# Alternating the two token halves between their banks in the dense stage

## The chip, the cores and the metric

The kernel runs on one core of a Trainium2 chip. TensorE multiplies, ScalarE and VectorE read its results out of eight accumulation banks (PSUM, 512 columns of f32 each), GpSimd and SyncE do side work and start DMAs. The metric is the time of one execution in microseconds, the median of several runs. Less is better.

## The reference

A batch of 256 tokens of 1024 values passes two transformer blocks. Cut to the matrix products and what stands between them:

```
h = x @ w_in                                   # first block: nine parts, 9216 columns
ua, va, za, qh, kh, vh, zb, ga, gb = split(h)
ya = gelu(ua) * mix(layer_norm(gelu(va))) * silu(za)
yb = rms_norm(diff_attention(rope(q), rope(k), v)) * silu(zb)
merged = sigmoid(ga) * (ya @ w_branch_a) + sigmoid(gb) * (yb @ w_branch_b)
ple = sigmoid(x @ w_ple_gate) * (p @ w_ple)
x = layer_norm(ALPHA * x + merged @ w_out + ple)

h = rms_norm(x) * (1 + scale_m) + shift_m      # second block
proj = h @ w_in_2                              # latents, fq, fk, fv, gates
merged = sigmoid(gate_a) * (o_mla @ w_o_mla) + sigmoid(gate_b) * (o_fox @ w_o_fox)
x = x + gate_m * (merged @ w_out_2)
h = rms_norm(x) * (1 + scale_f) + shift_f
x = x + gate_f * (shared(h) + routed(h))       # 64 experts, six for each token
return rms_norm(x)
```

All is float32, and the result is to hold that precision.

## The kernel before

The program has two stages. The dense stage does everything up to the last `x = x + gate_m * ...`. The expert stage behind it streams the weights of 64 experts, 3 MB each, and multiplies each with the few tokens that were routed to it.

The dense stage goes by names, each a product of all 256 tokens with 512 columns of a weight matrix (424 for c0): q0 q1 k0 k1 v0 v1 za0 za1 ua0 ... pg0 pg1 ple0 ple1 ba0 ba1 bb0 bb1 wo0 wo1 c0 fq fk fv g0 ... of0 of1 om0 om1 wp0 wp1. A weight matrix comes in loads of four blocks of 128 rows into a ring of five slots, and each load is cut into pieces of two blocks (list `pieces`). So a name of 1024 rows has four pieces, of0, of1, om0 and om1 have two, and ple0 and ple1 one each.

For float32 precision both operands are split in a high and a low part. ScalarE rounds a piece into its high part (`hl`, six buffers), VectorE subtracts to get the low part (`rlo`, in the slots' room). Three matmuls, here called passes, make one block of rows: high tokens by high weights, low tokens by high weights, high tokens by low weights. The tokens are the stationary operand, 128 at a time, so there are two halves, m = 0 and m = 1, each with a bank of its own. One piece for one half is six passes; a step is one piece for both halves, twelve passes.

The order of steps is in `steps_of`. Most names have both halves of a piece in one step. In the runs named in `BEHIND` (bb0 bb1, wo0 wo1, c0, om0 om1, wp0 wp1) the second half comes four (om: three) pieces behind the first. In such a run of eight pieces the steps 0 to 3 hold the first half alone, steps 4 to 7 both halves with different pieces, and steps 8 to 11 the second alone. c0 with its four pieces never has both in one step, and the om run has both in step 3 alone.

TensorE's part is `project`. A name's banks are `bank_of[name] + m`: names take the pair of banks 0, 1 and the pair 2, 3 in turn. Before its first piece a name waits until the name two before it has been emptied from the same bank (`two_before`, `evacuated`). After the last pass of each half of a step TensorE raises the counter `pe_w`; `pe_at` has its value for each piece and half. These wait on that counter:

- the emptying of a bank, by ScalarE (`keep`) or VectorE (`evac`), which waits for a half's last piece (`done`)
- the conversions, which wait for the second half of the piece six before (`both(g - NH)`)
- the loads, which wait for the second half of the last piece of the slot's load (`freed`)

VectorE and ScalarE have their own `project` functions. Each goes through its program in a fixed order, conversions and emptyings mixed, so an emptying can stand behind a conversion that is not ready. In the lagged runs VectorE empties a bank as soon as its name is done and goes on with what follows from it: for wo1 the layer norm, whose result TensorE needs for the transposing products `h_turn(0)`; for bb1 and om1 the sum (`merged`, `merged2`) that TensorE transposes within the run; for wp1 the sum and scale that `h3_turn(0)` transposes.

ple0 and ple1 are emptied by VectorE, by the function `ple`: for each half a product (a tensor_tensor from the bank) and then an addition (a scalar_tensor_tensor from `rbuf` to `rbuf`). The name ba0 comes two behind ple0 and takes its banks.

Of the kernel before, what the change touches and what calls it, by code (L numbers as in the profile page):

```python
# [76 lines left out]
def two_blocks(nc, D, out):  # L77
    ctx = ExitStack()
    with ctx:  # L79
        def sem(name):  # L80
            return ctx.enter_context(nc.semaphore(name))
# [81 lines left out]
        PS = [ctx.enter_context(nc.psum_tensor(f"ps{i}", [128, 512], F32)) for i in range(8)]  # L163
# [13 lines left out]
        def tok(m):  # L177
            return slice(128 * m, 128 * m + 128)
# [36 lines left out]
        loads, pieces, blocks, once = [], [], {}, {}  # L215
# [76 lines left out]
        for name in order:  # L292
# [3 lines left out]
            if name == names[0]:  # L296
                ps = [g for q in names for g in blocks[q]]
                steps_of[name] = []
                for s in range(len(ps) + lag):
                    t = sum(len(v) for v in steps_of.values())  # L300
                    halves = [(ps[s], 0)] if s < len(ps) else []
# [6 lines left out]
        block_of = {g: (name, n) for name in order for n, g in enumerate(blocks[name])}  # L308
# [3 lines left out]
        bank_of = {name: 2 * (n % 2) for n, name in enumerate(order)}  # L312
        two_before = {name: order[n - 2] if n > 1 else None for n, name in enumerate(order)}

        def hi_of(g):
            return hl[:, g % NH, 0:2 * pieces[g][2]].rearrange("p (k n) -> p k n", k=2)
# [50 lines left out]
        hi, lo, pe_w, mac = (sem(n) for n in ("hi", "lo", "pe_w", "mac"))  # L367
# [25 lines left out]
        def evacuated(name, m):  # L393
            ev = ev_v if (name, m) in ev_v.at else ev_a
            return ev.sem, ev.at[(name, m)]
# [422 lines left out]
        def _(e):  # L818
            w = Waits(e)

            def mm(o, l, r, start, stop):
                return e.matmul(o, l, r, start=start, stop=stop)  # L822

            def tr(o, i):
                n = i.shape[0]
                return e.transpose(o, i, ident[0:n, 0:n])  # L826
# [43 lines left out]
            def mod_sum(c):  # L870
                kind, h = c // 2, c % 2
                acc = macc[:, h, :]
                b = take(("mod", c))
                w.wait_ge(mac, 15 * in_turn.index(c) + 15)
                w.wait_ge(ones_set, 1)
                if kind in (2, 5):
                    x = mm(b[:, :], ones[:, :], acc, True, True)
                elif kind in (0, 1):
                    for f in range(4):
                        x = mm(b[:, f:f + 1], acc[:, 128 * f:128 * f + 128], ones[:, 0:1], True, True)  # L880
                else:
                    for k in range(8):
                        x = mm(b[64 * h:64 * h + 64, k:k + 1], acc.rearrange("p (q k) -> p k q", k=8)[:, k, :],
                               ones[:, 0:1], True, True)
                taken(x)

            def between(name, n):
                if n < len(HEADS_IN.get(name, ())):
                    head(HEADS_IN[name][n])
                for n0, s in PAIRS_IN[name][n] if name in PAIRS_IN else ():  # L890
                    pair(n0, s, 96 if n0 else 66, V2 if n0 else FV)

            def project(lead, L, ready, at={}):
                for name in names_of[lead]:
                    for c in MOD_SUM.get(name, ()):
                        mod_sum(c)
                four = len(blocks[lead]) == 4
                for s, (_, halves) in enumerate(steps_of[lead]):
                    for g, m in halves:
                        w.wait_ge(hi, g + 1)  # L900
                        w.wait_ge(lo, g + 1)
                        hi_g, lo_g = hi_of(g), pieces[g][3]
                        name, n = block_of[g]
                        o = PS[bank_of[name] + m][:, 0:pieces[g][2]]
                        if n == 0 and two_before[name]:
                            w.wait_ge(*evacuated(two_before[name], m))
                        for k in range(2):
                            kk = 2 * n + k
                            ready(m, kk)
                            mm(o, L[:, 0, kk, tok(m)], hi_g[:, k, :], kk == 0, False)  # L910
                            mm(o, L[:, 1, kk, tok(m)], hi_g[:, k, :], False, False)
                            x = mm(o, L[:, 0, kk, tok(m)], lo_g[:, k, :], False, kk == 2 * len(blocks[name]) - 1)
                        x.then_inc(pe_w, 1)
                    if s == 1 and four:
                        between(lead, 0)
                    if s in at:
                        at[s]()
                between(lead, 1 if four else 0)
# [76 lines left out]
            for name in ("q0", "q1", "k0", "k1", "v0"):  # L995
                project(name, L0, x_ready)
            turn("qT", lambda m, j: ROT[:, m, 128 * j:128 * j + 128], lambda m, j0: w.wait_ge(roped, 2))
            for name in ("v1", "za0"):
                project(name, L0, x_ready)
            turn("kT", lambda m, j: ROT[:, m, 128 * j:128 * j + 128], lambda m, j0: w.wait_ge(roped, 4))  # L1000
            for name in ("za1", "ua0", "ua1", "va0", "va1", "zb0", "zb1"):
                project(name, L0, x_ready)
            wsT = slot(once["wsT"])[:, 0:1024].rearrange("p (g t) -> p g t", g=8)
            for m in range(2):
                for c in range(2):
# [3 lines left out]
                    for j in range(4):  # L1009
                        g = 4 * c + j  # L1010
                        x = mm(b[:, 128 * j:128 * j + 128], wsT[:, g, :], VA[:, m, 128 * g:128 * g + 128], True, True)
# [24 lines left out]
            for m in range(2):  # L1036
                b = take(("lT", m))
                w.wait_ge(lat_set, 1)
                for j in range(3):
                    x = tr(b[:, 128 * j:128 * j + 128], PR[:, m, 128 * j:128 * j + 128])  # L1040
# [1547 lines left out]
```

## Time and profile before

| | us |
|---|---|
| median of 3 runs | 1091.11 |
| lowest and highest | 1090.81, 1092.13 |
| the profiled execution | 1089.95 |
| its span, first to last instruction | 1088.2 |
| TensorE busy | 1033.8 (95%) |
| VectorE busy | 563.1 (52%) |
| ScalarE busy | 394.3 (36%) |

The span is what the trace shows; the profiled execution is 1.75 us longer than it. Matmuls overlap: the next starts before the one ahead of it has ended, so their pace is read from the distance of their starts. The granted clock of a stretch is a share of TensorE's 2.4 GHz: 1.00 or 0.50. Accumulation banks stand as `ps` in all rows of the trace, without their number.

### The profile page before, as it was taken

How to read it: one execution, taken by the hardware profiler on the slowest of the kernel's cores; microseconds unless marked ns; L12 is line 12 of the kernel's file. 1: busy time of each engine (PE TensorE's matmuls, PEld its weight loads, DVE VectorE, ACT ScalarE, POOL GpSimd, SP SyncE). 2: the span in 40 equal slices, each digit the busy share in tenths (PEclk: the TensorE clock that was granted, in tenths of full speed). 3: DMA queues.
4: the chain of work that ended last, by engine and by line, in shares of the span. 5: the costliest groups of instructions: out<-in, count | busy, mean ns of one | idle time of the engine just before them, and what ended most of it. 6: DMA issues, size and time to landing. Idle time of an engine off the chain costs nothing. (4 is left out here: it accounts for less than half of the span.)

```text
span 1088.2 us, 12949 instructions
## 1 busy us (share of the span) xinstructions
PE 1033.8 (95%) x5024; PEld 688.3 (63%) x5024; DVE 563.1 (52%) x1018; ACT 394.3 (36%) x678; POOL 387.3 (36%) x309
## 2 busy tenths in 40 slices
PE   8999998999999899999999999999999899999993
PEld 7888886878788787788877444444444344444351
DVE  5899678676976876666666222222222222222214
ACT  5646665365434644657334111111212111211102
POOL 1499999689970398198000000000000000000000
PEclk9999999899999999899999999999999999999997
DMA  9766666566765567355289799999999999999991
GB/s 325 255 216 232 209 196 213 191 216 240 254 210 173 182 218 266 125 170 179 88 281 413 270 419 415 416 415 416 418 415 416 414 416 416 417 415 416 417 380 39
DMA packets 91917, 320.63 MB, mean 295 GB/s; under 512 B 8752, under 2 KB 11856, under 8 KB 75216
## 3 DMA queue, kind: packets, MB, share of 16 engines
q1 hardware_dynamic: 83904, 290.90, 70.0%
q0 software_dynamic: 7664, 28.37, 7.8%
q8 instruction: 41, 0.67, 0.3%
q10 hardware_dynamic: 288, 0.52, 0.1%
q14 instruction: 20, 0.16, 0.0%
HBM read 318.72 MB, written 1.05 MB: 294 GB/s over the span
## 5 line engine op out<-in xcount | busy, mean ns | idle before, releaser
L822 PE MATMUL ps<-hl,L 128*128 128x512 f32 (+1 forms) x1216 | 383.0, 396 | 7.0 <-issue 3.2
L822 PEld LDWEIGHTS ps<-hl,L 128*128 128x128 f32 x1216 | 226.9, 190 | 58.5 <-issue 9.7
L1673 DVE TENSOR_TENSOR rlo<-ring,hl 128x1024 fp32r<-128x1024 f32 (+1 forms) x154 | 216.2, 1425 | 83.9 <-ACT hl L1274 83.5
L822 PE MATMUL ps<-slots_all,xe 128*64 128x512 f32 (+1 forms) x1088 | 234.4, 570 | 9.6 <-DMA slots_all<-in_w_exp_up 8.7
L822 PE MATMUL ps<-rlo,L 128*128 128x512 f32 (+1 forms) x608 | 238.0, 391 | 0.0
L1274 ACT ACTIVATE hl<-ring 128x1024 fp32r<-128x1024 f32 (+1 forms) x154 | 159.5, 1054 | 151.7 <-PE ps L822 100.8
L811 POOL CAST two<-ident 64x128 fp32r<-64x128 f32 x64 | 18.9, 295 | 484.2 <-PE ps L822 482.7
L764 POOL TENSOR_SCALAR mring<-mring,st 128x512 f32<-128x512 f32 x84 | 176.7, 2104 | 1.6
L822 PEld LDWEIGHTS ps<-slots_all,xe 128*64 128x64 f32 x1088 | 80.2, 137 | 141.4 <-issue 135.9
L822 PEld LDWEIGHTS ps<-rlo,L 128*128 128x128 f32 x608 | 115.0, 189 | 24.0
L766 POOL TENSOR_TENSOR macc<-macc,mring 128x512 f32<-128x512 f32 x84 | 124.2, 1478 | 7.0
L1679 DVE SCALAR_TENSOR_TENSOR hh<-ps,gslot,hh 128x256 f32<-128x256 f32 x32 | 15.5, 484 | 208.8 <-ACT hh L1274 208.8
L822 PE MATMUL ps<-slots_all,hh 128*64 128x512 f32 x512 | 122.1, 595 | 0.0
L1274 ACT ACTIVATE hh<-ps 128x256 f32<-128x256 f32 x64 | 24.7, 386 | 220.6 <-PE ps L822 212.4
L1274 ACT ACTIVATE yy<-ps 128x512 fp32r<-128x512 f32 x64 | 34.9, 595 | 171.3 <-PE ps L822 171.3
L822 PEld LDWEIGHTS ps<-slots_all,hh 128*64 128x64 f32 x512 | 41.5, 138 | 70.6 <-issue 65.2
L1673 DVE TENSOR_TENSOR yy<-ps,yy 128x512 fp32r<-128x512 f32 x64 | 41.3, 686 | 55.2 <-ACT yy L1274 55.2
L822 PE MATMUL ps<-yy,ppt 128*128 128x512 f32 x256 | 65.5, 398 | 3.5 <-DVE yy L1673 3.5
L1676 DVE TENSOR_SCALAR ppt<-ps,cols 128x128 fp32r<-128x128 f32 x64 | 19.5, 347 | 92.0 <-PE ps L822 92.0
L822 PEld LDWEIGHTS ps<-yy,ppt 128*128 128x128 f32 x256 | 48.3, 190 | 15.1 <-DVE yy L1673 4.5
L762 POOL TENSOR_SCALAR macc<-mring,st 128x512 f32<-128x512 f32 x12 | 23.8, 1983 | 92.5 <-PE ps L822 87.3
L786 POOL DMA_DIRECT2D mring<-in_w_mod x48 | 36.7, 764 | 41.3 <-PE ps L822 27.6
(218 smaller groups left out, 925.2 us busy)
## 6 DMA issues: line engine op xcount, KB each, us to landing
slots_all<-in_w_exp_gate SPq DMA_DIRECT2D x64, 1024.0 KB, 22.6
slots_all<-in_w_exp_up SPq DMA_DIRECT2D x64, 1024.0 KB, 21.5
slots_all<-in_w_exp_down SPq DMA_DIRECT2D x64, 1024.0 KB, 22.3
ring<-in_w_in SPq DMA_DIRECT2D x48, 1024.0 KB, 5.4
mring<-in_w_mod POOLq DMA_DIRECT2D x48, 512.0 KB, 4.3
ring<-in_w_out SPq DMA_DIRECT2D x8, 1024.0 KB, 5.1
ring<-in_w_ple_gate SPq DMA_DIRECT2D x4, 1024.0 KB, 6.6
ring<-in_w_branch_a SPq DMA_DIRECT2D x4, 1024.0 KB, 5.3
```

The source lines that it names most:

```text
L762: e.tensor_scalar(acc, v, s, None, ALU.mult).then_inc(mac, 1)
L764: e.tensor_scalar(v, v, s, None, ALU.mult).then_inc(mac, 1)
L766: e.tensor_tensor(acc, acc, v, ALU.add).then_inc(mac, 1)
L786: e.dma_start(mring[:, n % 2, :].rearrange("p (a b) -> p a b", a=2), kn(D["w_mod"], 512 * c, 512 * c + 512)[:, 2 * q:2 * q + 2]).then_inc( ...
L811: x = e.tensor_copy(two[s, i % 2, :].rearrange("p (e c) -> p e c", e=2), spread(ident[s, 64 * r + 2 * i:64 * r + 2 * i + 2], 64))
L822: return e.matmul(o, l, r, start=start, stop=stop)
L1274: return e.activation(o, i, f, **kw)
L1673: return e.tensor_tensor(o, a, b, op)
L1676: return e.tensor_scalar(o, a, s1, s2, op0, op1) if op1 is not None else e.tensor_scalar(o, a, s1, None, op0)
L1679: return e.scalar_tensor_tensor(out=o, in0=a, scalar=s, in1=b, op0=op0, op1=op1)
```

## The change

The six passes of a piece were issued for one half, then for the other. Now every pass of the first half is followed by the same pass of the second. All bank waits of a step's halves now stand ahead of its first pass, and the counter is raised for both halves at the end of the step. Where a step has one half, its order is as it was.

```diff
                     for g, m in halves:
                         w.wait_ge(hi, g + 1)
                         w.wait_ge(lo, g + 1)
-                        hi_g, lo_g = hi_of(g), pieces[g][3]
                         name, n = block_of[g]
-                        o = PS[bank_of[name] + m][:, 0:pieces[g][2]]
                         if n == 0 and two_before[name]:
                             w.wait_ge(*evacuated(two_before[name], m))
-                        for k in range(2):
-                            kk = 2 * n + k
-                            ready(m, kk)
-                            mm(o, L[:, 0, kk, tok(m)], hi_g[:, k, :], kk == 0, False)
-                            mm(o, L[:, 1, kk, tok(m)], hi_g[:, k, :], False, False)
-                            x = mm(o, L[:, 0, kk, tok(m)], lo_g[:, k, :], False, kk == 2 * len(blocks[name]) - 1)
-                        x.then_inc(pe_w, 1)
+                    for k in range(2):
+                        for a, of_hi in ((0, True), (1, True), (0, False)):
+                            for g, m in halves:
+                                name, n = block_of[g]
+                                kk = 2 * n + k
+                                ready(m, kk)
+                                x = mm(PS[bank_of[name] + m][:, 0:pieces[g][2]], L[:, a, kk, tok(m)],
+                                       (hi_of(g) if of_hi else pieces[g][3])[:, k, :], kk == 0 and a == 0 and of_hi,
+                                       kk == 2 * len(blocks[name]) - 1 and not of_hi)
+                                if k == 1 and not of_hi:
+                                    x.then_inc(pe_w, 1)
```

TensorE, the first step of ba0, as it stood (`ps0` and `ps1` are the banks of the two halves, `ev_v` is the counter of banks that VectorE has emptied):

```order
L822 MATMUL ps0<-hl_67,L1_70 128x512 [waits ev_v,lo,hi]
L822 MATMUL ps0<-hl_67,L1_70 128x512
L822 MATMUL ps0<-rlo_68,L1_70 128x512
L822 MATMUL ps0<-hl_67,L1_70 128x512 x2
L822 MATMUL ps0<-rlo_68,L1_70 128x512
L822 MATMUL ps1<-hl_67,L1_70 128x512 [waits ev_v]
L822 MATMUL ps1<-hl_67,L1_70 128x512
L822 MATMUL ps1<-rlo_68,L1_70 128x512
L822 MATMUL ps1<-hl_67,L1_70 128x512 x2
L822 MATMUL ps1<-rlo_68,L1_70 128x512
```

The same step now:

```order
L822 MATMUL ps0<-hl_67,L1_70 128x512 [waits ev_v,lo,hi]
L822 MATMUL ps1<-hl_67,L1_70 128x512
L822 MATMUL ps0<-hl_67,L1_70 128x512
L822 MATMUL ps1<-hl_67,L1_70 128x512
L822 MATMUL ps0<-rlo_68,L1_70 128x512
L822 MATMUL ps1<-rlo_68,L1_70 128x512
L822 MATMUL ps0<-hl_67,L1_70 128x512
L822 MATMUL ps1<-hl_67,L1_70 128x512
L822 MATMUL ps0<-hl_67,L1_70 128x512
L822 MATMUL ps1<-hl_67,L1_70 128x512
L822 MATMUL ps0<-rlo_68,L1_70 128x512
L822 MATMUL ps1<-rlo_68,L1_70 128x512
```

The wait of the seventh pass has gone into the wait of the first.

TensorE, from step 7 of the bb run to the start of step 8, now (`ps2` is bb1's bank for the first half, `ps1` bb0's for the second, `ps3` bb1's for the second; what ended step 7 before is its six passes into `ps1`, and bb1's first half was done ahead of them):

```order
L822 MATMUL ps2<-hl_67,L0_69 128x512
L822 MATMUL ps1<-hl_67,L0_69 128x512
L822 MATMUL ps2<-hl_67,L0_69 128x512
L822 MATMUL ps1<-hl_67,L0_69 128x512
L822 MATMUL ps2<-rlo_68,L0_69 128x512
L822 MATMUL ps1<-rlo_68,L0_69 128x512
L822 MATMUL ps3<-hl_67,L0_69 128x512 [waits ev_v]
```

The last pass into `ps2` stands right ahead of the last into `ps1`. The orders of the other engines are unchanged.

## Rows read from the trace of the kernel before

**Rows 1.** The page, costliest groups: count, busy us, mean ns, idle before.
```profile
L822 PE MATMUL ps<-hl,L 128*128 128x512 f32 (+1 forms) x1216 | 383.0, 396 | 7.0 <-issue 3.2
...
L822 PE MATMUL ps<-rlo,L 128*128 128x512 f32 (+1 forms) x608 | 238.0, 391 | 0.0
```

**Rows 2.** Order of time, TensorE, step of k0: start, us taken, instruction, count, idle before.
```profile
40.19 0.62 PE L822 MATMUL ps<-hl,L 128*128 128x512 f32 x2
...
40.87 0.62 PE L822 MATMUL ps<-hl,L 128*128 128x512 f32 x2
...
41.55 0.62 PE L822 MATMUL ps<-hl,L 128*128 128x512 f32 x2
...
42.23 0.62 PE L822 MATMUL ps<-hl,L 128*128 128x512 f32 x2
```

**Rows 3.** Order of time, TensorE, from ple1's last pass into ba0's first step.
```profile
289.90 0.39 PE L822 MATMUL ps<-rlo,pL 128*128 128x512 f32 x1
291.82 0.69 PE L822 MATMUL ps<-hl,L 128*128 128x512 f32 x2 [1.53 <-ACT hl L1274]
...
293.27 0.62 PE L822 MATMUL ps<-hl,L 128*128 128x512 f32 x2
```

**Rows 4.** Order of time, VectorE, the emptying of ple0's two banks.
```profile
290.98 0.69 DVE L1673 TENSOR_TENSOR bs<-ps,bs 128x512 f32<-128x512 f32 x1
291.70 0.69 DVE L1679 SCALAR_TENSOR_TENSOR rbuf<-rbuf,bs 128x512 f32<-128x512 f32 x1
292.31 0.68 DVE L1673 TENSOR_TENSOR bs<-ps,bs 128x512 f32<-128x512 f32 x1
```

**Rows 5.** Order of time, TensorE, at the ends of the lagged runs.
```profile
330.30 0.39 PE L822 MATMUL ps<-rlo,L 128*128 128x512 f32 x1
...
331.66 0.39 PE L822 MATMUL ps<-rlo,L 128*128 128x512 f32 x1
...
338.55 0.70 PE L822 MATMUL ps<-hl,L 128*128 128x512 f32 x2 [0.17 <-DVE L L1673]
...
364.47 3.50 PE L822 MATMUL ps<-bs,rbuf 128*128 128x128 f32 x16 [2.88 <-DVE bs L1676]
...
541.39 1.03 PE L826 MATMUL ps<-ident,bs 128*128 128x128 f32 x8
...
568.71 1.05 PE L826 MATMUL ps<-ident,xp 128*128 128x128 f32 x8
```

**Rows 6.** Order of time, VectorE, in the same runs.
```profile
331.66 0.68 DVE L1673 TENSOR_TENSOR bs<-ps,bs 128x512 f32<-128x512 f32 x1
...
337.72 1.28 DVE L1673 TENSOR_TENSOR L<-ps,L 128x512 fp32r<-128x512 f32 x2
...
356.52 1.04 DVE L1673 TENSOR_TENSOR rlo<-ring,hl 128x848 fp32r<-128x848 f32 x1 [3.56 <-ACT hl L1274]
357.48 0.68 DVE L2096 SCALAR_TENSOR_TENSOR rbuf<-ps,rbuf 128x512 f32<-128x512 f32 x1
...
539.59 0.69 DVE L1673 TENSOR_TENSOR bs<-bs 128x512 f32<-128x512 f32 x1
...
565.61 0.75 DVE L1676 TENSOR_SCALAR xp<-rbuf,st 128x1024 f32<-128x1024 f32 x1
```

**Rows 7.** Stretches: bounds, length, TensorE busy (instructions), granted clock, DMA share, GB/s.
```profile
289.70:293.10 3.40, 1.87 (x9) 1.00 1.03 387
361.60:364.80 3.20, 0.33 (x3) 1.00 1.04 371
364.80:368.20 3.40, 3.40 (x19) 0.50 0.43 165
598.00:1061.00 463.00, 449.13 (x2141) 1.00 0.99 405
```

**Rows 8.** Order of time, TensorE, dense passes at the lower clock.
```profile
10.10 1.05 PE L822 MATMUL ps<-hl,L 128*128 128x512 f32 x2
10.96 0.63 PE L822 MATMUL ps<-rlo,L 128*128 128x512 f32 x1
```

## The prediction, made before the changed kernel ran

> **What bounds the kernel now.** I read the costliest groups first. TensorE is busy 95% of the span, and its 1216 passes with the high weight parts and 608 with the low ones are the dense stage [rows 1]; 24 more, of the two ple names, stand in smaller groups: 1848 in all, the last of them just ahead of the transposes at 568.71 us [rows 5]. A pass is one matmul of 512 columns. Its duration (0.39 us) overlaps the next one, so what counts is the distance of starts, which the order of time on TensorE gives: three passes in 0.68 us, 0.227 us each [rows 2]. TensorE hardly waits in this stage, so its end is the number of passes times 0.227 us, plus the waits, plus what a lower clock costs. The expert stage behind it is held by the weight stream: from 598 to 1061 us the DMA engines are 0.99 busy at 405 GB/s [rows 7]. That stream cannot run ahead of the dense stage, because its first slots are room that dense pieces free, and the later ones wait for expert work that needs the dense stage's result. So I let a delay of dense work travel to the end one to one. Nothing between is paced by a clock of its own: ring loads, conversions and evacuations all wait in the end for TensorE's counter.
>
> **Does alternating change a pass?** The 1848 passes, their weight loads and the order of sums in each bank stay. Only the neighbour changes. A pass already follows one into another bank once in six: in [rows 2] the step of k0 starts at 40.19, its second half (other bank) at 41.55. From 40.19 to 40.87 all three neighbours share a bank; from 40.87 to 41.55 the last of the three changes it. Both take 0.68 us. So a change of bank costs 0.00 us, to the 0.01 us that the rows resolve. Half a hundredth either way on 1848 passes would be -9 to +9 us; I take 0, which is what the row shows, and keep the rest as a small chance. The Trainium skill ("TensorE: Matmul & The Clock Gate", Back-to-back issue gap) gives 216 ns for a lone gap at 512 columns, 11 ns under the trace; were that gap the price of sharing a bank, 1848 of them would bring about 20 us by an estimate from that page. But the bank change in the rows does not show any of it.
>
> **Waits moved forward.** The new code collects the bank waits of both halves ahead of the first pass; so far the second half's stood ahead of pass 7. That hoists a wait over six passes, 1.36 us of cover. It matters only where the second bank is emptied late. I went through the names for one that starts close behind the reader of its banks, and found it at ba0. ba0 uses the banks of ple0, and ple1 in between is only 12 passes long. In the trace TensorE ends ple1 at 289.90 + 0.39, and starts ba0 at 291.82 [rows 3]. The row names ScalarE, but that conversion belongs to a later piece; VectorE's tensor_tensor that empties ple0's first bank runs 290.98 to 291.67 [rows 4], and 0.15 us later ba0 starts. Another release by VectorE takes 0.19 us (337.72 plus half of 1.28, to the start at 338.55) [rows 5, 6]. VectorE empties the second bank from 292.31 to 292.99, behind an addition of its own at 291.70 [rows 4]. The old order needs it for pass 7 at 293.27, so it is free [rows 3]. The new order needs it at pass 1: start 292.99 + 0.15 = 293.14 instead of 291.82, **+1.32 us**. VectorE is not slowed or sped by this, since the work it does there (rlo before, its own additions behind) has its inputs. The bounds: 0 if the release is of another kind, +1.45 if the wait reaches to pass 7's old start. I take 1.32. At the other names the readers finish many us ahead (in the lagged runs the banks were left a whole name ago), so 0.
>
> **First half finished later.** The counter for a half's last pass rises in turn; the second half's stays at pass 12, the first's moves from pass 6 to 11: 5 x 0.227 = 1.13 us later. Ring slots and the high and low buffers are freed by the second half only, so no load and no conversion moves. What moves is the emptying of the first bank. In unlagged names one engine then does both banks in a row: the first starts 0.23 us ahead of pass 12's end and takes 0.69 at most [rows 4], so the second is late by 0.69 - 0.23 = 0.46 us at most, which the engines' idle time takes up. The costly case would be a lagged run, where the first half's result heads a chain that TensorE waits for. The four places [rows 5, 6]:
> - bb: VectorE comes to bb1's first bank at 331.66, far behind pass 6 (330.30), because a low part was due first. Pass 11 will start 0.23 before 331.66 and end at 331.82; with 0.03 to react, 331.85: +0.19. From here VectorE works without a gap to the L at 337.72 that TensorE waits for at 338.55. So **+0.19 us**; in other orders of events 0 to 1.13.
> - wo: VectorE comes to wo1's first bank at 357.48, held by the c0 weights whose conversion it awaits at 356.52. Pass 11 ends near 355.9. **0**; with the weights there early, up to 1.13, since TensorE waits for that chain until 364.47.
> - om: VectorE idles for pass 6 here. Its pair ends at 539.59 + 0.69 = 540.28, will end at 541.41. The turn at 541.39 needs it only for its second four transposes, about 0.45 us in, and the low part behind it slips by some 0.03: I take **+0.05 us**.
> - wp: the chain ends at 565.61 + 0.75 = 566.36; 1.13 later it is 567.49, still ahead of the transposes at 568.71. **0**.
>
> **The clock.** The stall at ba0 grows from 1.53 to 2.85 us (290.29 to 293.14). A stall of 2.88 us ahead of 364.47 [rows 5] holds TensorE at 0.33 us of work from 361.6 to 364.8, at a granted clock of 1.00, and then the clock is 0.50 (1.2 GHz) for 3.4 us [rows 7]. The stall of 1.53 us at ba0 leaves 1.87 us of work in its stretch, and no such fall [rows 7]. The new one leaves 1.87 - 1.32 = 0.55. At the lower level two passes take 10.96 - 10.10 = 0.86 us, 0.43 each [rows 8]. If 3.4 us of dense passes run there, 8 passes take 3.4 instead of 1.8 us: **+1.6 us**. Behind 364.8 the slow stretch fell on small work; here it would fall on full passes, with nothing to hide it. Bounds: 0, and twice that, 3.2. I take one fall, as the row nearest in length (2.88) had it; it need not come in every execution, hence the large chance without it.
>
> **Sum.** 1.32 + 0.19 + 0.05 = 1.56; with the fall 3.16. The profiled execution took 1089.95 us (span 1088.2 and 1.75 around it): 1093.1. The median of the runs is 1.16 above it, 1091.11: **1094.3 us**. A measurement tells about 0.2% here, 2.2 us, so up to 1093.3 counts as no change.
>
> **Rivals.**
> - B, stall without a fall. The wait is hoisted but the clock holds: 1091.11 + 1.56 = 1092.7, range 1091.9 to 1093.4, no change for a measurement. For it: one row pair is thin evidence for a fall.
> - C, not slower: the delay is given back. The wait at ba0 is taken up by a later one that depends on something else than TensorE, in the first place the 2.88 us ahead of 364.47 [rows 5]. Its chain hangs on the c0 weights, awaited at 356.52 [rows 6]. If that load were paced by the DMA engines and not by the slot that TensorE frees, all 1.5 us would vanish: 1091.1, range 1090.2 to 1091.9. Against it: the load's slot is freed by a piece of wo itself. The same time comes out if the release at ba0 is not the bank's.
> - D, passes get shorter. Then each ns per pass is 1.85 us; 3 ns give 1091.1 + 1.6 - 5.5 = 1087. Against: [rows 2].
> - E, more falls. With two low stretches more, or a longer one, 1091.1 + 1.6 + 2 x 1.6 = 1095.9 and beyond, to 1098; it decides if TensorE pauses briefly at many bank changes. A rule of the Trainium skill speaks for this (same page, A second HAM failure mode: psum-queue depth-cycling): cycling through banks each iteration made TensorE idle so often for a moment that its clock swung. By that rule the new order is the risky one. The trace has bank changes every 1.36 us without a pause [rows 2], so I give it little.
>
> **Chances.** Forecast (stall and one fall, own range 1093.4 to 1095.4) 0.44; B 0.28; C 0.12; D 0.06; E 0.10. Slower by over 0.2%: 0.44 + 0.10 + 0.02 of B = 0.56. Faster: 0.06 of D + 0.01 = 0.07. Within: the other 0.37. The range from 1090.6 to 1096.4 leaves out D and most of E and takes in C.
>
> **What would show it.** In the new profile: ba0's first pass 1.3 us later against ple1's end than before, released right behind the second emptying by VectorE; 0.68 us for three passes everywhere; a granted clock of 0.50 in the 3.4 us behind ba0's start and passes of 0.43 there; the wait ahead of wo0 about 0.2 longer; the waits at the turns of the wo, om and wp runs as before; the weight stream starting later by the sum. I am wrong if ba0 starts when it did, if three passes take something else than 0.68 us, or if a stall of wo, om or wp grows by a us.

## The result, and the profile after

| | before | after |
|---|---|---|
| median of the runs of this comparison, us | 1091.43 (7 runs) | 1095.97 (7 runs) |
| lowest and highest | 1090.24, 1093.23 | 1092.28, 1098.19 |
| the profiled execution | 1089.95 | 1096.45 |
| its span | 1088.2 | 1094.7 |
| mean granted clock of TensorE | 0.981 | 0.976 |

The changed kernel is slower by a ratio of 1.0039 [1.0023, 1.0056], that is by 4.3 us [2.5, 6.1]. A second series, run with the experiments below, gave 1.0024 [1.0009, 1.0039], that is 2.6 us [1.0, 4.3]. The forecast had been 3.2 us.

TensorE's order of time at the place of [rows 3] (start, us taken, instruction, count, idle before and what ended it), after:

```profile
293.08 0.62 PE L822 MATMUL ps<-rlo,pL 128*128 128x512 f32 x2
296.55 1.17 PE L822 MATMUL ps<-hl,L 128*128 128x512 f32 x4 [2.85 <-DVE bs L1675]
297.56 0.62 PE L822 MATMUL ps<-rlo,L 128*128 128x512 f32 x2
```

and VectorE's at the place of [rows 4]:

```profile
294.14 0.69 DVE L1675 TENSOR_TENSOR bs<-ps,bs 128x512 f32<-128x512 f32 x1
294.86 0.94 DVE L1681 SCALAR_TENSOR_TENSOR rbuf<-rbuf,bs 128x512 f32<-128x512 f32 x1
295.73 0.68 DVE L1675 TENSOR_TENSOR bs<-ps,bs 128x512 f32<-128x512 f32 x1
```

The idle time ahead of ba0 has grown from 1.53 to 2.85 us. The row now names VectorE's product, and it is the second one: 295.73 + 0.68 = 296.41, and 0.14 us later ba0 starts. The first had been done at 294.83. With the old order ba0 would have started 0.14 us behind it. So in this execution the moved wait costs 1.57 us, and the stall without it would have been 1.28.

The passes themselves, as in [rows 2], in a step of k0:

```profile
40.68 1.07 PE L822 MATMUL ps<-hl,L 128*128 128x512 f32 x4
41.59 0.61 PE L822 MATMUL ps<-rlo,L 128*128 128x512 f32 x2
42.04 1.07 PE L822 MATMUL ps<-hl,L 128*128 128x512 f32 x4
```

Six passes, now each in the other bank than the one ahead, take 42.04 - 40.68 = 1.36 us: 0.227 each, as before.

Four more places of TensorE, in order of time: the sums behind the turn of ya, the first pass of wo0 (before: 0.17 idle, [rows 5]), the transposing products of `h_turn(0)` (before: 2.88), and the product of the query latents, which stands inside fv and has no wait in the trace of [rows 5]:

```profile
249.50 2.08 PE L822 MATMUL ps<-ones,macc 128*64 128x1 f32 x16 [0.41 <-DVE L L1675]
...
343.50 0.70 PE L822 MATMUL ps<-hl,L 128*128 128x512 f32 x2 [0.37 <-DVE L L1675]
...
369.54 2.82 PE L822 MATMUL ps<-bs,rbuf 128*128 128x128 f32 x16 [3.00 <-DVE bs L1678]
...
422.60 1.85 PE L822 MATMUL ps<-ring,rt 128*128 128x384 f32 x5 [1.92 <-DVE st L1678]
...
575.02 1.05 PE L826 MATMUL ps<-ident,xp 128*128 128x128 f32 x8
```

The last row answers to 568.71 in [rows 5]: the dense stage ends 6.31 us later. The span is 6.5 us longer, so what comes behind is the same: 1094.7 - 575.0 = 519.7, before 1088.2 - 568.7 = 519.5. In all ten traces of this study that rest is between 519.4 and 519.8.

But 6.3 us in one execution are not the change alone. The stage as one stretch (bounds, length, TensorE, its weight loads, VectorE, ScalarE and GpSimd busy, granted clock, DMA share, GB/s), before:

```profile
0.00:568.70 568.70, 547.61 (x2692) 456.00 (x2693) 420.86 (x650) 302.85 (x480) 367.83 (x244) 0.98 0.63 211
```

and after:

```profile
0.00:575.00 575.00, 548.74 (x2692) 456.17 (x2693) 424.42 (x650) 301.25 (x480) 362.67 (x244) 0.97 0.62 208
```

Busy time grew by 1.1 us and idle time by 5.2 us (21.1 to 26.3). Of the 5.2, 1.32 stand ahead of ba0, 0.25 behind the turn of ya, 0.20 ahead of wo0, 0.12 ahead of `h_turn(0)` and 1.92 in fv: 3.81. Most of the rest is in small waits: 0.8 in the first 60 us, 0.3 ahead of 229.05, 0.2 between 370 and 386. The 1.92 turn up in a trace of the kernel before too (below), so they are no proof against the change.

Half of the 6.3 us was there before ba0. The last pass of ple1 ends at 293.70, before at 290.29: 3.4 us later. Of these, 0.55 come up in the first 60 us. 0.85 come where a low stretch of the clock was 10.2 us long before (from 187.3) and 13.7 after (from 186.3). 0.3 are the wait ahead of 229.05, and 0.25 the one behind the turn of ya. The other 1.4 come behind that turn, where the changed kernel's clock is 0.50 for 3.4 us from 251.2, on full passes. Before:

```profile
249.52 0.73 PE L822 MATMUL ps<-hl,L 128*128 128x512 f32 x2
```

and after, four passes at 0.47 us from start to start:

```profile
251.51 2.07 PE L822 MATMUL ps<-hl,L 128*128 128x512 f32 x4
253.38 1.05 PE L822 MATMUL ps<-rlo,L 128*128 128x512 f32 x2
```

Six of the ten traces have that stretch: both of the changed kernel, neither of the kernel before. But hoist_only has it with the old order and the old wait of 0.16 us, and only_last is without it at 0.41. So it isn't tied to the longer wait.

The stretch from ba0's start, after; the order of its columns is the same:

```profile
292.10:295.50 3.40, 1.60 (x7) 0.94 (x6) 3.33 (x4) 0.47 (x1) 3.07 (x2) 1.00 1.05 400
295.50:298.90 3.40, 2.35 (x10) 1.99 (x11) 3.37 (x5) 1.53 (x2) 3.22 (x3) 1.00 1.06 394
...
598.00:1061.00 463.00, 449.89 (x2164) 209.98 (x2164) 113.70 (x268) 73.92 (x158) 17.98 (x61) 1.00 1.00 407
```

The clock stayed at 1.00 behind the longer stall at ba0. The forecast had it fall. The last row answers to that of the weight stream in [rows 7], 0.99 and 405 GB/s before.

### The profile page after: what moved, and what is told of

Read it like the earlier page. It is cut to its first block and busy times, and to the rows that moved or that the text cites. A ratio compares the mean times of both kernels' runs of the same rounds, so it can differ in the third digit from the quotient of the medians.

```text
span 1094.7 us, 12977 instructions
## 1 busy us (share of the span) xinstructions
PE 1035.9 (95%) x5024; PEld 690.8 (63%) x5024; DVE 566.5 (52%) x1018; ACT 392.8 (36%) x678; POOL 382.2 (35%) x309
## 5 line engine op out<-in xcount | busy, mean ns | idle before, releaser
L822 PE MATMUL ps<-hl,L 128*128 128x512 f32 (+1 forms) x1216 | 342.6, 399 | 8.7 <-issue 3.3
L822 PEld LDWEIGHTS ps<-hl,L 128*128 128x128 f32 x1216 | 228.4, 191 | 60.7 <-issue 10.2
L1675 DVE TENSOR_TENSOR rlo<-ring,hl 128x1024 fp32r<-128x1024 f32 (+1 forms) x154 | 219.2, 1443 | 85.5 <-ACT hl L1276 85.0
L822 PE MATMUL ps<-rlo,L 128*128 128x512 f32 (+1 forms) x608 | 195.2, 392 | 0.0
L764 POOL TENSOR_SCALAR mring<-mring,st 128x512 f32<-128x512 f32 x84 | 171.8, 2045 | 1.6
```

Of the source, the lines that this page charges most:

```text
L764: e.tensor_scalar(v, v, s, None, ALU.mult).then_inc(mac, 1)
L1675: return e.tensor_tensor(o, a, b, op)
```

## Experiments

Each kernel was timed against the kernel before on the same chip. The 35 runs of the kernel before had a median of 1093.15 us in the first series (hoist_only, not_ba0, only_last, inner_steps) and 1093.39 in the second, which ran on another chip. A number of one profile is given as such: two executions of one kernel differ by some us, as before_again will show.

### hoist_only: the wait alone

The order of before is kept; only the wait for ba0's second bank is taken ahead of pass 1.

```diff
                 for s, (_, halves) in enumerate(steps_of[lead]):
+                    if lead == "ba0" and s == 0:
+                        for m in range(2):
+                            w.wait_ge(*evacuated(two_before[lead], m))
                     for g, m in halves:
```

> The order of before everywhere, but ba0's first step waits for both of its banks ahead of pass 1. Theory 1 (the hoisted wait at ba0 is most of the +4.5 us): the stall ahead of ba0 is 2.85 us instead of 1.53, no other stall grows for that reason, and the time is before +1.3, or up to +3 with a clock fall behind the stall. Theory 2 (the late first halves are most of it): the same stall of 2.85, but the time within +1.3 of before, so well under after. Either way three passes stay at 0.68 us.

Measured: 1095.42 us, ratio 1.0014 [1.0000, 1.0029], that is 1.5 us [0, 3.2]. TensorE:

```profile
292.74 0.39 PE L822 MATMUL ps<-rlo,pL 128*128 128x512 f32 x1
295.67 1.19 PE L822 MATMUL ps<-hl,L 128*128 128x512 f32 x2 [2.54 <-DVE bs L1676]
296.65 0.63 PE L822 MATMUL ps<-rlo,L 128*128 128x512 f32 x1
```

One moved wait, with no pass alternating, makes most of the stall: 2.54 us, where 2.85 had been expected. VectorE's two products end at 293.99 and 295.56, so the moved wait costs 1.57 us here too. The time is inside what either expectation allows and does not tell them apart; the next kernel does. Here the clock did fall. The stretch behind ba0's start:

```profile
295.20:298.60 3.40, 2.94 (x7) 2.39 (x8) 3.33 (x5) 1.82 (x2) 3.27 (x3) 0.51 1.05 395
```

### not_ba0: everything but ba0's first step

From the changed kernel; ba0's first step goes one half after the other, each with its wait where it was.

```diff
+                    alternate = not (lead == "ba0" and s == 0)
+                    for group in ([halves] if alternate else [[half_] for half_ in halves]):
```

(The waits and passes of a step then loop over `group` in place of `halves`. The next two kernels differ from this one in the condition alone.)

> The order of after everywhere, but ba0's first step in the old order with its waits where they were. Theory 1: the stall ahead of ba0 is back at 1.5 us and the time falls by 1.3 to 3 us against after, to before +1.5 or so. Theory 2: it stays within 1.3 us of after, at before +3; the stalls of after ahead of the mod sum behind the turn of ya (0.41 against 0.16) and ahead of the query latents in fv (1.92 against none) stay.

Measured: 1092.99 us, ratio 0.9997 [0.9981, 1.0012], -0.3 us [-2.1, 1.3]. Twelve passes out of 1848 put back in the old order take the loss away, within what can be measured. Against hoist_only, timed in the same series, the median is 2.4 us lower. TensorE:

```profile
247.16 2.08 PE L822 MATMUL ps<-ones,macc 128*64 128x1 f32 x16 [0.41 <-DVE L L1677]
...
290.91 0.62 PE L822 MATMUL ps<-rlo,pL 128*128 128x512 f32 x2
292.82 0.70 PE L822 MATMUL ps<-hl,L 128*128 128x512 f32 x2 [1.29 <-DVE bs L1677]
...
339.91 0.71 PE L822 MATMUL ps<-hl,L 128*128 128x512 f32 x2 [0.38 <-DVE L L1677]
```

and VectorE's first product:

```profile
291.99 0.69 DVE L1677 TENSOR_TENSOR bs<-ps,bs 128x512 f32<-128x512 f32 x1
```

The stall is 1.29 us, and ba0 starts 0.14 us behind the end of that product (291.99 + 0.69 = 292.68). The 0.41 and 0.38 of the changed kernel are still there, so these two are not from ba0.

### only_last and inner_steps: the late first half against mere alternation

only_last alternates only the steps that hold a name's last piece for the first half, where alternating delays the emptying (ba0's first step is not one of them). inner_steps alternates all others but ba0's first: some 1160 passes, counted from the names (29 names of four pieces with three such steps of 12, less ba0's first, 24 of of0 and of1, and 108 in the lagged runs).

```diff
+                    alternate = any(m == 0 and block_of[g][1] == len(blocks[block_of[g][0]]) - 1 for g, m in halves)
```

> The old order, except in the steps that hold the last piece of a name's first half, which alternate. So first halves end late as in after, and no wait is hoisted at ba0. Theory 1: before +0.2 to +0.5, stall ahead of ba0 1.5. Theory 2: before +2 to +4, with the stall behind the turn of ya at 0.41 and a stall in fv.

> Alternating in all steps with two halves except ba0's first and those that hold the last piece of a name's first half. Some 1200 passes change their neighbour, no first half ends late, no wait is hoisted where it matters. Both theories: the same as before within 0.5 us, ba0's stall 1.5, three passes in 0.68 us. A rival (a change of bank costs or gives something by itself, by pauses or by the pace) would show as over 2 us either way or as three passes off 0.68.

Measured: only_last 1093.91 us, 1.0008 [0.9993, 1.0022], 0.9 us [-0.8, 2.4]; inner_steps 1092.89 us, 1.0006 [0.9989, 1.0023]. The times tell neither from no change. The stalls ahead of ba0 were 1.64 and 1.03 us, where 1.5 had been expected of both. What alternation does is seen in the traces. only_last:

```profile
248.75 2.08 PE L822 MATMUL ps<-ones,macc 128*64 128x1 f32 x16 [0.41 <-DVE L L1677]
...
340.52 0.69 PE L822 MATMUL ps<-hl,L 128*128 128x512 f32 x2 [0.38 <-DVE L L1677]
```

inner_steps, with a step of k0 ahead of the same two places:

```profile
44.21 1.07 PE L822 MATMUL ps<-hl,L 128*128 128x512 f32 x4
45.12 0.62 PE L822 MATMUL ps<-rlo,L 128*128 128x512 f32 x2
45.57 1.07 PE L822 MATMUL ps<-hl,L 128*128 128x512 f32 x4
...
247.09 2.08 PE L822 MATMUL ps<-ones,macc 128*64 128x1 f32 x16 [0.16 <-DVE L L1677]
...
339.43 0.70 PE L822 MATMUL ps<-hl,L 128*128 128x512 f32 x2 [0.15 <-DVE L L1677]
```

So 0.41 and 0.38 come with the late first halves, 0.16 and 0.15 without, and alternation by itself costs nothing that is seen: 1.36 us for six passes, no pauses, and a ratio whose interval holds 1. The clock is at 0.50 for 27.3 us of this dense stage, as in the first trace of the kernel before. The Trainium skill ("TensorE: Matmul & The Clock Gate", A second HAM failure mode: psum-queue depth-cycling) tells of a kernel that went through banks each iteration, was idle for a moment between its groups of matmuls, and whose clock swung between its two levels. These 1160 passes show no such idle moments, and they add no time at the lower clock.

### after_again and before_again: the two kernels once more

> The changed kernel once more, for a second trace of it. If a clock fall follows ba0's stall in some executions and not in others, this trace may have it where the first had none; the stall itself is 2.85 us again. The time is before +3 to +6. The stall in fv (1.92 us in the first trace) stays if it comes from where TensorE stands against GpSimd's loads, and is gone if it was chance.

> The kernel before once more, for a second trace. Stalls of 1.53 us ahead of ba0, 0.16 behind the turn of ya, 2.88 ahead of the transposing products, none in fv. The stretches at the lower clock may differ from the first trace: if their number and length differ between executions of one program, a difference of a few us in one profiled execution says little about the change.

Measured: after_again 1095.08 us, 1.0024 [1.0009, 1.0039]; before_again 1093.96 us, 1.0011 [0.9994, 1.0027], which shows what the comparison makes of no change. The medians of the two are only 1.1 us apart, so this series alone is weak evidence for a loss, and after_again stayed below the 3 to 6 us that had been expected. TensorE of after_again:

```profile
291.19 0.62 PE L822 MATMUL ps<-rlo,pL 128*128 128x512 f32 x2
294.67 2.05 PE L822 MATMUL ps<-hl,L 128*128 128x512 f32 x4 [2.86 <-DVE bs L1675]
296.52 1.06 PE L822 MATMUL ps<-rlo,L 128*128 128x512 f32 x2
...
573.47 1.05 PE L826 MATMUL ps<-ident,xp 128*128 128x128 f32 x8
```

and its stretches (columns as above):

```profile
290.70:294.10 3.40, 1.11 (x5) 0.56 (x3) 3.33 (x4) 2.00 (x2) 3.02 (x3) 1.00 1.05 392
294.10:297.50 3.40, 2.83 (x7) 2.30 (x8) 3.33 (x5) 0.00 (x0) 3.27 (x3) 0.50 1.05 393
297.50:300.90 3.40, 3.40 (x17) 2.80 (x16) 3.37 (x5) 1.06 (x1) 3.32 (x3) 1.00 0.12 43
```

The stall is the same 2.86 us, and this time the fall behind it is there: 0.50 for 3.4 us, four passes in 2.05 us instead of 1.17. The first twelve passes take 4.13 us from start to start, against 2.84 in the first trace: the fall costs 1.3 us. after_again does not have fv's stall. before_again has that one, which had not been expected of it, and ends its dense stage 1.9 us behind the first trace of the same kernel (568.71, [rows 5]):

```profile
418.20 6.37 PE L822 MATMUL ps<-ring,rt 128*128 128x384 f32 x18 [1.92 <-DVE st L1676]
...
570.61 1.05 PE L826 MATMUL ps<-ident,xp 128*128 128x128 f32 x8
```

before_again's stall ahead of ba0 is 0.63 us, not 1.53. There ple1's first pass had waited 1.16 us for ScalarE, which was emptying pg1's first bank, so TensorE came to ba0 later.

### after_early and before_early: both banks emptied first

If ba0's start is set by VectorE's emptying of ple0's banks, then emptying them sooner removes the loss, and more: the stall that was there before. VectorE does both products ahead of the low parts of ba0's third and fourth piece, which it had been doing first, and both additions behind the products. The same edit is made to the changed kernel and to the one before.

```diff
+                        if g == blocks["ba0"][2]:
+                            ple0_out()
                         w.wait_ge(hi, g + 1)
...
+            def ple0_out():
+                for m in range(2):
+                    o = PL[:, m, half(0)]
+                    done("ple0", m)
+                    w.wait_ge(*evacuated("pg0", m))
+                    tt(o, PS[bank_of["ple0"] + m][:, :], o, ALU.mult).then_inc(ev_v.sem, 1)
+                for m in range(2):
+                    o, r = PL[:, m, half(0)], B(0)[:, m, half(0)]
+                    w.wait_ge(*evacuated("ple0", m))
+                    w.wait_ge(x_in, 16)
+                    mine(stt(r, r, ALPHA, o, ALU.mult, ALU.add))
...
-            for c in range(2):
-                project(f"ple{c}", ple(c))
+            project("ple0")
+            project("ple1", ple(1))
```

> The changed kernel, with VectorE emptying ple0's two banks first and adding afterwards, and this ahead of the low parts of ba0's third and fourth piece. It takes away what the hoisted wait waits for. Theory 1: no stall ahead of ba0 (under 0.2 us against 2.85), the time falls by 2.7 us or more against after, to before +0 to +2. Theory 2: the stall goes too, and the time stays above before by 2 us and more.

> The kernel before with the same earlier emptying of ple0. The stall of 1.53 us ahead of ba0 goes; before -1.5 us if stalls are not given back later, 0 if they are. This is also the test that TensorE's time in the dense stage carries to the end one to one, and the candidate to beat both kernels.

Measured: after_early 1090.90 us, ratio 0.9980 [0.9963, 0.9997]; before_early 1091.37 us, 0.9979 [0.9967, 0.9992]. Both beat both kernels, and the two orders of passes now give the same time. For the old order that is 2 us, for the new one 4.2 us (1090.90 against 1095.08). VectorE of after_early:

```profile
289.64 1.29 DVE L1675 TENSOR_TENSOR bs<-ps,bs 128x512 f32<-128x512 f32 x2
290.84 2.38 DVE L1681 SCALAR_TENSOR_TENSOR rbuf<-rbuf,bs 128x512 f32<-128x512 f32 x2
```

and its TensorE, with no idle time ahead of ba0 (the second row), and the end of the stage:

```profile
291.26 0.62 PE L822 MATMUL ps<-rlo,pL 128*128 128x512 f32 x2
291.72 1.07 PE L822 MATMUL ps<-hl,L 128*128 128x512 f32 x4
...
570.02 1.05 PE L826 MATMUL ps<-ident,xp 128*128 128x128 f32 x8
```

Both products are over at 290.93, ahead of ple1's last pass. The dense stage of before_early ends at 565.40, 3.3 us sooner than in the trace of before; again a single execution, of which the ratio bears out 2.3 us.

## Why the prediction was right, step by step

- **The wait at ba0, +1.32 us.** The mechanism is shown: 2.85 and 2.86 us in place of 1.53, released 0.14 us behind the second product. hoist_only makes 2.54 of it by the wait alone, not_ba0 has 1.29, and with the banks emptied early it is gone. It is the one term that a timed pair tells apart: hoist_only is 2.4 us above not_ba0, which alternates everywhere else. That the difference came out at 1.32 is luck. With the old order the stall was 1.53, 0.63, 1.29, 1.64 and 1.03 us in five traces, as VectorE and TensorE happened to stand. What the moved wait adds is the distance between the ends of the two products: 1.57 to 1.59 us in six of the eight traces where an addition stands between them, 1.32 in the two (before and only_last) where that addition took 0.69 us and not 0.94 or more. The forecast was read from one of the two.
- **No hoisted wait at the other names, 0.** Neither trace of the changed kernel shows one. It is not safe, though: in before_again and before_early ple1's first pass waits 1.16 and 0.21 us for ScalarE, and there the new order would ask for pg1's second bank too.
- **The first half later.** bb was put at +0.19 and measured 0.20 (0.17 to 0.37; 0.38 in not_ba0 and only_last). `h_turn(0)`, put at 0, had 3.00 and 2.79 us against 2.88; in before_again it was 2.98, so the 0.1 are no change. om was put at +0.05: the low part behind the turn did not slip, and the wait in that run was 0.65 us in both traces, so 0.00. wp was put at 0 and is 0: no idle time ahead of the last transposes.
- **A step that failed** is "so the second is late by 0.69 - 0.23 = 0.46 us at most, which the engines' idle time takes up". At the turn of ya it does not. ga0's banks are emptied by ScalarE, and what it does next is to round the transposed ya into its high part in the stationary buffer `L`. VectorE then makes the low part, which TensorE waits for. ScalarE, before:

```profile
244.28 0.60 ACT L1274 ACTIVATE bs<-ps 128x512 f32<-128x512 f32 x1 [0.24 <-PE ps L822]
...
245.64 0.60 ACT L1274 ACTIVATE bs<-ps 128x512 f32<-128x512 f32 x1 [0.76 <-PE ps L822]
246.13 2.06 ACT L1274 ACTIVATE L<-ps 128x512 fp32r<-128x512 f32 x4
```

and after:

```profile
247.14 1.09 ACT L1276 ACTIVATE bs<-ps 128x512 f32<-128x512 f32 x2 [1.37 <-PE ps L822]
248.12 2.07 ACT L1276 ACTIVATE L<-ps 128x512 fp32r<-128x512 f32 x4
```

  Before, the two emptyings stand apart, each behind its half, with idle time ahead of both. After, both follow pass 11 in one go. TensorE's transposes behind ga0's last pass start at 245.44 before and 247.18 after, so the rounding into `L` starts 0.69 and then 0.94 us behind them: +0.25, and TensorE's wait goes from 0.16 to 0.41. It is the same in all five traces with late first halves and in none of the others. The bound of 0.46 was right and the cover was not there. The sum should have been 1.57 + 0.20 + 0.25 = 2.02 ahead of the clock.
- **The clock, +1.6 us.** Right in kind, not in each execution. Of three traces with a stall of 2.5 us or more ahead of ba0, two show 0.50 in the next 3.4 us and one (the changed kernel's first) shows 1.00; of the seven with 1.64 us or less, none. After the fall TensorE's four passes took 2.05 instead of 1.17 us, and the price was 1.3 us, not 1.6: the first half us of the low stretch fell on the stall. So it is the price of some executions; how often it is paid three traces don't tell. The forecast also left out that the clock falls elsewhere. Over the dense stage, behind its first 7 us, it is low for 27.3 and 23.9 us in the two traces of the kernel before, 34.1 and 30.7 in the two of the changed one, and 20.5 to 37.5 in the other six.
- **A pass keeps its length.** Shown: 0.227 us in both orders, and inner_steps at 1.0006 [0.9989, 1.0023]. The interval still leaves room for 2.5 us, some 2 ns on each of 1160 passes; the rows leave none.
- **One to one to the end.** Shown: the rest behind the dense stage is 519.4 to 519.8 us in ten traces whose dense stage ends anywhere from 565.4 to 575.0.
- **The rivals.** B (no fall, 1.56 us) is what the first trace looks like at ba0; by the times the loss of the first series lies above it, and that of the second holds both B and the forecast. C (given back) fell: `h_turn(0)` waits as long as before, behind a start 5 us later. D (shorter passes) fell with inner_steps. Of E, the cause it named (TensorE pausing at many bank changes) fell with inner_steps too. But its sign, two low stretches of 3.4 us more, is there in the changed kernel's first trace (34.1 against 27.3 us), and the measured 1095.97 lies above the forecast's own range (1093.4 to 1095.4) and at the foot of E's. not_ba0, with no loss, has 30.7 us too, so the traces don't say that the change brings them.

The size agrees with the sum within wide intervals: 2.0, or 3.3 with the fall, against 4.3 [2.5, 6.1] and 2.6 [1.0, 4.3]. That 3.2 had been forecast rests in part on terms that were off in opposite ways: the wait too small, the turn of ya left out, the fall too dear and not in each execution.

The 1.92 us in fv hang on a weight load. These are ScalarE's conversions that wait for the load, and VectorE's rows that TensorE waits for, after:

```profile
415.79 2.01 ACT L1276 ACTIVATE hl<-ring 128x1024 fp32r<-128x1024 f32 x2 [5.24 <-DMA ring<-in_w_in]
420.87 1.63 DVE L1678 TENSOR_SCALAR rt<-ps,cols 128x128 f32<-128x128 f32 x6
```

VectorE first makes the low parts of these conversions, so its rows start 5.08 us behind them, and TensorE's product 6.81 us behind them. The same 6.80 to 6.82 us stand in all ten traces. In seven TensorE has to wait 1.66 to 2.61 us for it, one of the kernel before among them; in before's first, in hoist_only and in after_again its passes fill the time.

**What stays open** is why that load lands sooner or later, and why the clock has more low stretches in one execution than in another. Whether the changed kernel has more of them is not shown: two traces of each kernel can't tell. If it had, that would be a part of the loss beside the three terms. No experiment was made on either.

## What to carry to other kernels

When two accumulation groups are interleaved, all their bank waits collect at the first pass; look for the names that start closest behind the reader of their banks, since there the hoisted wait costs. Read the distance between the two emptyings from more than one trace. Interleaving also delays the earlier group's end by all but one pass, so two emptyings that were spread now come in a burst, and whatever their engine owes to TensorE next slips. Where an engine empties two banks, let what frees the banks go ahead of follow-up work and of conversions that are needed later: the two together were worth 2 us here in the old order of passes and 4 in the new. No run parts them. By the rows the conversions are the larger: five low parts ahead of the products took 6.77 us in not_ba0, three took 4.09 in after_early, and an addition takes 0.7 to 0.95.

## What the runs showed of the hardware that was not expected

- A change of bank between two matmuls of 512 columns costs nothing that the trace resolves: 1.36 us for six passes both with one change and with six.
- The clock's falls differ between executions of one program. The kernel before had low stretches of 3.4, 10.2, 3.4 and 10.2 us in its dense stage in one execution; in the other 10.2, 3.4, 3.4 and 6.8, and in the changed kernel a stall of 2.86 us was followed by 0.50, one of 2.85 by 1.00.
- A stall of some us can be in one execution and not in the next: 1.92 us in fv, present in one trace and absent in the other, for each of the two kernels. It goes with the landing of one weight load, 6.8 us ahead of the product in all ten traces.
